# Two hybrid transformer blocks in float32: another order for VectorE and ScalarE at the front and the tail of each mixing

## The reference

```python
# per layer, both blocks
x = x + 0.5 * swiglu(rmsnorm(x), w_gate, w_up, w_down)      # width 2816
x = x + mixing(rmsnorm(x)) @ w_out
x = x + 0.5 * swiglu(rmsnorm(x), w_gate2, w_up2, w_down2)

# mixing of block 1: neighbourhood attention (8 heads) and gated linear attention (4 heads, two directions)
log_g = log_sigmoid(code @ w_gate + b_gate) / 16            # a cumulative sum of it is the decay
o = concat(rmsnorm(na(q, k, v)), rmsnorm(o_fwd + o_bwd) * silu(r))

# mixing of block 2: forgetting attention, dilated attention with rotary positions, HGRN2
log_f = logaddexp(log(lb), log(1 - lb) + log_sigmoid(z))    # z: the projection hf
k = (1 - lb) * sigmoid(-z);  q = silu(q_raw)                # q_raw: the projection hq
o = concat(fox, dilated, rmsnorm(hgrn2(q, k, v, log_f)) * sigmoid(g))
```

## Time and profile before

| | |
|---|---|
| three runs | 2106.34, 2108.96 and 2109.08 us; median 2108.96 |
| profiled execution, its own time | 2110.61 us |
| its span, first to last instruction | 2108.8 us |
| PE busy | 2048.7 us (97%) |
| DVE busy, ACT busy | 1310.0 us (62%), 1058.2 us (50%) |
| mean granted TensorE clock | 0.988 |
| DMA | 169 GB/s from HBM over the span |

### The profile page before, as it was taken

One profiled execution on the slowest core, in us unless ns is written; L12 is line 12 of the kernel. 1 busy time (PEld: TensorE's weight loads), 2 busy tenths in 40 slices (PEclk: granted clock), 3 DMA queues, 4 the chain that ended last, 5 costly groups with the idle time before them and its releaser, 6 DMA issues.

```text
span 2108.8 us, 26738 instructions
## 1 busy us (share of the span) xinstructions
PE 2048.7 (97%) x11144; PEld 1714.2 (81%) x11144; DVE 1310.0 (62%) x1532; ACT 1058.2 (50%) x1278; POOL 56.6 (3%) x72
## 2 busy tenths in 40 slices
PE   7999999999999999999999999999999999999998
PEld 5888877888888887788788888878888889887886
DVE  5655866555655686655565568765556556976554
ACT  4444565444544556544454456654454445565443
POOL 3200004000000000000000000000000000000000
PEclk9999999999999999999999999999999999999999
DMA  8654336555555433555455543345545554335551
GB/s 279 214 195 162 140 112 178 185 187 192 179 181 194 156 131 110 183 181 195 164 177 182 193 156 136 116 169 191 183 176 198 182 184 175 121 121 182 188 181 59
DMA packets 52217, 357.81 MB, mean 170 GB/s; under 512 B 6592, under 2 KB 7008, under 8 KB 9600
## 3 DMA queue, kind: packets, MB, share of 16 engines
q1 hardware_dynamic: 48960, 350.25, 46.6%
q0 software_dynamic: 2416, 5.51, 1.3%
q10 hardware_dynamic: 720, 0.34, 0.1%
HBM read 355.02 MB, written 1.05 MB: 169 GB/s over the span
## 4 chain that ended last, share of the span: by engine, by line
PE 88%; DVE 6%; ACT 3%; DVEq 1%; issue 1%; DMA 0%; ACTq 0%
PE bank L360 82%; DVE w_lo L1087 2%; PE bank L464 2%; PE bank L520 1%; PE bank L404 1%; ACT w_hi L747 1%; PE bank L601 1%; DVE h_lo L1104 1%; PE bank L566 1%; DMA cos_sin<-positions 0%; PE bank L587 0%; ACT h_hi L767 0%; DVEq L1275 0%; ACTq L920 0%; ACT arena L935 0%
## 5 line engine op out<-in xcount | busy, mean ns | idle before, releaser
L1087 DVE TENSOR_TENSOR w_lo<-raw,w_hi 128x2048 fp32r<-128x2048 f32 x332 | 762.7, 2297 | 387.8 <-ACT w_hi L747 387.4
L747 ACT ACTIVATE w_hi<-raw 128x2048 fp32r<-128x2048 f32 x332 | 634.3, 1911 | 270.9 <-PE bank L360 260.7
L360 PE MATMUL bank<-w_hi,h_hi 128*128 128x512 f32 x1536 | 611.7, 398 | 7.1 <-DVE w_lo L1087 4.1
L360 PE MATMUL bank<-w_hi,h_lo 128*128 128x512 f32 x1536 | 600.4, 391 | 0.0
L360 PE MATMUL bank<-w_lo,h_hi 128*128 128x512 f32 x1536 | 599.7, 390 | 0.0
L360 PEld LDWEIGHTS bank<-w_hi,h_hi 128*128 128x128 f32 x1536 | 289.4, 188 | 71.0 <-DVE w_lo L1087 10.2
L360 PEld LDWEIGHTS bank<-w_hi,h_lo 128*128 128x128 f32 x1536 | 289.0, 188 | 62.1
L360 PE MATMUL bank<-w_hi,act_hi 128*128 128x512 f32 x832 | 330.4, 397 | 6.3 <-DVE act_lo L1384 6.3
L360 PEld LDWEIGHTS bank<-w_lo,h_hi 128*128 128x128 f32 x1536 | 289.8, 189 | 56.5
L360 PE MATMUL bank<-w_lo,act_hi 128*128 128x512 f32 x832 | 326.1, 392 | 0.0
L360 PE MATMUL bank<-w_hi,act_lo 128*128 128x512 f32 x832 | 326.1, 392 | 0.0
(11 more groups left out here) (195 smaller groups left out, 1460.7 us busy)
## 6 DMA issues: line engine op xcount, KB each, us to landing
raw<-stream SPq DMA_DIRECT2D x332, 1024.0 KB, 4.8
arena<-rpb POOLq DMA_DIRECT2D x32, 96.0 KB, 9.3
x<-xt SPq DMA_DIRECT2D x4, 256.0 KB, 7.0
arena<-final_gain POOLq DMA_DIRECT2D x2, 512.0 KB, 4.5
out<-x SPq DMA_DIRECT2D x4, 256.0 KB, 2.8
arena<-c_level POOLq DMA_DIRECT2D x1, 384.0 KB, 3.4
arena<-code_w POOLq DMA_DIRECT2D x2, 128.0 KB, 3.6
arena<-c_att POOLq DMA_DIRECT2D x1, 256.0 KB, 5.0
```

The costliest lines, as they stand in the source:

```text
L360: last = mm(o, a, r, start=start and n == 0, stop=stop and n == len(pairs) - 1)
L747: fn(w_hi[u % SLOTS][:, :], raw[u % RAW][:, :], ACT.Copy).then_inc(hi_done, 1)
L1087: tt(w_lo[u % SLOTS][:, :], raw[u % RAW][:, :], w_hi[u % SLOTS][:, :].bitcast(F32), ALU.subtract).then_inc(lo_done, 1)
```

## The change

No instruction is added or left out but for drains and semaphores. The order changes:

1. Block 1, front: the logits (`gate_logits`) come ahead of the eviction of gq, the rest (`gate_sums`) behind the split of unit 3. The split of unit 4 moves behind `span_scale(0)` and `span_decay(1)`.
2. Block 2, front: turns 0 to 4 of DVE are one function, `hgrn_front`. Evictions and splits lie between the steps of the gate's chain, and the splits of units 6 and 7 behind all of it. ACT's order follows.
3. Tails: the split of unit i+3 in turn 10 or 13 comes early on both engines; `recurrence_rs` finishes its first half before the second; the transposes of item 7 go into the output unit, after its sixth of eight rows; block 1's `norm_sums` goes from after the fourth row of r = 1 to after the second.
4. Start of an FFN (six of the eight): `split(back 0)` stands between the pieces 1 and 2 of `turned_lo`, and `mean_square` behind piece 3.

```diff
@@ PE, mixing: output units
-                        between = None
+                        between = {}
                         if b == 1 and r == 0:
-                            between = lambda: recurrence_norm(b, L)
+                            between[0, 3] = lambda: recurrence_norm(b, L)
                         if b == 0 and r == 1:
-                            between = lambda: norm_sums(L)
+                            between[0, 1] = lambda: norm_sums(L)
+                        if TURN_AFTER[b].get(nunits + r) == 7:
+                            between[1, 1] = lambda: transposes(b, L, 7)
@@ ACT, recurrence_rs
                 for i in range(2):
                     fn(cum[:, 2 * i:2 * i + 2, :].rearrange("p a b -> p (a b)"), PX[i][:, :], ACT.Ln, bias=eps[:, :], scale=1.0 / P)
-                act.drain().then_inc(o_ln, 1)
-                for i in range(2):
+                    if i == 0:
+                        act.drain()
+                    else:
+                        act.drain().then_inc(o_ln, 1)
                     fn(cum[:, 2 * i:2 * i + 2, :], cum[:, 2 * i:2 * i + 2, :], ACT.Exp, scale=-0.5).then_inc(o_rs, 1)
@@ ACT, mixing
-                    late = i >= RECURRENCE_AFTER[b]
+                    late = i > RECURRENCE_AFTER[b]
...
+                    if b == 1 and i == 1:
+                        softplus(dec[:, :, :], qk2[:, 1, :, :], LAYERS + 2 * L + 1)
                     if not late:
                         split(mix_use(b, L, i + 3))
...
-                    if b == 1 and i == 2:
+                    if b == 1 and i in (1, 2):
+                        pair = slice(2 * (i - 1), 2 * i)
+                        act.wait_ge(evicted, plain_no(b, L, i + 1))
+                        fn(sig_tmp[1][:, pair, :], qk2[:, 0, pair, :], ACT.Exp, scale=-1.0)
+                    if b == 1 and i == 3:
                         act.wait_ge(gsilu, L + 1)
-                        fn(qk2[:, 1, :, :], qk2[:, 1, :, :], ACT.Exp)
                         fn(qks2[:, 0, :, :], qks2[:, 0, :, :], ACT.Exp)
                         act.drain()
                         fn(qks2[:, 0, :, :], qks2[:, 0, :, :], ACT.Ln, bias=1.0).then_inc(rg_done, 1)
-                    if name in ("hq0", "hq1"):
-                        pair = slice(2 * (i - 2), 2 * (i - 2) + 2)
-                        act.wait_ge(evicted, plain_no(b, L, i))
-                        fn(sig_tmp[1][:, pair, :], qk2[:, 0, pair, :], ACT.Exp, scale=-1.0)
-                    if name == "hq1":
+                        act.wait_ge(z_less, L + 1)
+                        fn(qk2[:, 1, :, :], qk2[:, 1, :, :], ACT.Exp).then_inc(z_exp, 1)
                         sigmoid(sig_tmp[1]).then_inc(sig_ready, 1)
@@ DVE, start of an FFN
-                    turned_lo(b, L, 2 * j, [1, 2, 3])
+                    turned_lo(b, L, 2 * j, [1])
+                    split(use_of("back", 0))
+                    turned_lo(b, L, 2 * j, [2, 3])
+                    mean_square(v)
                 else:
                     turned_lo(b, L, 2 * j, [0, 1, 2, 3])
-                mean_square(v)
-                split(use_of("back", 0))
+                    mean_square(v)
@@ DVE, gates
-            def gates(b, L):
-
-                tmp = qks1.rearrange("p a b t -> p (a b) t")
+            def gate_logits(L):
+
                 dve.wait_ge(z_ready, L + 1)
                 for c in range(4):
-                    ts(dec[:, c, :], PD[3 * (c // 2)][:, (c % 2) * T:(c % 2 + 1) * T], gain(b, L, "bias", c), None, ALU.add)
+                    ts(dec[:, c, :], PD[3 * (c // 2)][:, (c % 2) * T:(c % 2 + 1) * T], gain(0, L, "bias", c), None, ALU.add)
                 dve.drain().then_inc(logit_ready, 1)
+
+            def gate_sums(L):
+
+                tmp = qks1.rearrange("p a b t -> p (a b) t")
                 dve.wait_ge(softplus_ready, L + 1)
@@ DVE, in place of turns 0 to 4 of block 2
+            def hgrn_front(L):
+
+                z, mx, mn = qk2[:, 1, :, :], qks2[:, 1, :, :], qks2[:, 0, :, :]
+                evict(1, L, 0)
+                evict(1, L, 1)
+                dve.drain().then_inc(logit_ready, 1)
+                split(mix_use(1, L, 3))
+                dve.wait_ge(softplus_ready, LAYERS + 2 * L + 2)
+                stt(dec[:, :, :], z, 0.0, dec[:, :, :], ALU.min, ALU.subtract)
+                dve.drain()
+                tt(z, dec[:, :, :], z, ALU.subtract).then_inc(z_less, 1)
+                evict(1, L, 2)
+                split(mix_use(1, L, 4))
+                tt(dec[:, :, :], dec[:, :, :], wide(lb_all[:, L, 1, :, None], P, 4, T), ALU.add)
+                dve.drain()
+                tt(mx, dec[:, :, :], wide(lb_all[:, L, 0, :, None], P, 4, T), ALU.max)
+                evict(1, L, 3)
+                tt(mn, dec[:, :, :], wide(lb_all[:, L, 0, :, None], P, 4, T), ALU.min)
+                dve.drain()
+                tt(mn, mn, mx, ALU.subtract).then_inc(gsilu, 1)
+                split(mix_use(1, L, 5))
+                dve.wait_ge(rg_done, L + 1)
+                tt(mx, mx, mn, ALU.add)
+                dve.drain()
+                scans(4, mx, cum)
+                dve.wait_ge(z_exp, L + 1)
+                tt(z, z, wide(lb_all[:, L, 2, :, None], P, 4, T), ALU.mult)
+                dve.wait_ge(sig_ready, L + 1)
+                tt(qk2[:, 0, :, :], qk2[:, 0, :, :], sig_tmp[1], ALU.mult)
+                dve.drain()
+                base = decay_A[64:P, 0, 0, 0:64]
+                v.memset(bass.AP(tensor=base.tensor, offset=base.offset, ap=[base.ap[0], [4 * T + P, 2], [T, 4], [1, 64]]), 0.0)
+                span_scale(1, L, 0)
+                span_decay(1, L, 1)
+                evict(1, L, 4)
+                split(mix_use(1, L, 6))
+                split(mix_use(1, L, 7))
@@ DVE, mixing
-                    late = i in SPAN_AFTER[b] or item is not None or (b == 1 and i >= 3) or r >= 0
+                    opens = b == 0 and i + 1 in SPAN_AFTER[0] and SPAN_AFTER[0][i + 1] == 0
+                    late = i in SPAN_AFTER[b] or item is not None or r >= 0 or opens
+                    if b == 0 and i == 0:
+                        gate_logits(L)
...
                     if b == 0 and i == 0:
-                        gates(b, L)
...
+                        gate_sums(L)
...
+                    if i == RECURRENCE_AFTER[b]:
+                        split(mix_use(b, L, i + 3))
...
-                    if late:
+                    if late and i != RECURRENCE_AFTER[b]:
                         split(mix_use(b, L, i + 3))
```

More of the change, by code:

```diff
@@ L388, in row, with row_unit @@
                 return wide(PD[i][:, :], a_hi[:, kk, tok], a_lo[:, kk, tok], slice(kk * D + half * 512, kk * D + half * 512 + 512), u, start, stop)
-            def row_unit(u, a_hi, a_lo, first, between=None):
+            def row_unit(u, a_hi, a_lo, first, between={}):
                 ready(u)
@@ L395, in row_unit @@
                         last = row(u, i, kk, a_hi, a_lo, first and kk == 0, False)
-                    if kk == 0 and between is not None:
-                        between()
-                last.then_inc(used, 1)
+                        if (kk, i) == (1, 3):
+                            last.then_inc(used, 1)
+                        if (kk, i) in between:
+                            between[kk, i]()
             def turn(nn, source, half, t):
@@ L465, in turn_act, with down @@
                     last.then_inc(at_ready, 1)
-                def down(g, between=None):
+                def down(g, between={}):
                     pe.wait_ge(alo_ready, ffn_no(b, L, j, g) + 1)
@@ L677, in slot @@
                 item, turned = ITEM_AFTER[b].get(i), TURN_AFTER[b].get(i)
-                if turned is not None:
+                if turned is not None and turned < 7:
                     transposes(b, L, turned)
@@ L1447, in mixing @@
                     forget_sums(L)
-                for i in range(nunits + UNITS_OUT - 2):
+                    hgrn_front(L)
+                for i in range((0, 5)[b], nunits + UNITS_OUT - 2):
                     r = i - nunits
@@ L1487, in mixing @@
                         fox_tables(L)
[L1488 removed]
+                    if opens:
                         span_scale(b, L, 0)
```

39 lines of the change are left out of this document (3 added, 36 removed).

## The result

The changed kernel takes 2076.22 us (median of four executions, 2073.69 to 2077.44), the kernel before 2107.8 beside it. The ratio is 0.985, with a 95% interval of 0.9837 to 0.9863. The forecast was 2078, with a range of 2067 to 2090. The profiled execution has an own time of 2076.41 us and a span of 2074.6, against 2110.6 and 2108.8: 34.2 us less by either. The medians are 31.6 us apart; four executions of one kernel lie up to 3.8 us apart.

A forecast was written before the change was run, and what follows sets the result against it. PE, busy 97% of the span, was taken as the bound, gaining only at waits or low clock. Terms 10.2 + 4.4 + 11.8 + 1.4 + 3.6 = 31.4 us off 2110.6, adjusted to the median, gave 2078; range 2067 to 2090.

The forecast's parts named there:

- The new wait at the first `heads`: Block 1's front: PE waits 1.7 us behind DVE's decay and ACT's evictions and copy, taking back part of the gain.
- the fall from 3.2 to 2.2 us of lead: Block 2's front, after span step 1: PE is 3.2 us ahead of before, DVE only 2.2; 2.2 is counted.
- All six dips: Half-clock stretches of 6.83 us behind three long PE waits, each in two layers; their removal counted as 15.2 us before residues.
- rival (a): New PE waits in both fronts and block 1's tails pull the clock down again; 13.6 us for all six, 2091; chance 0.20.
- a border between 0.7 and 2.5 us: Length of PE wait above which the clock dips: none seen behind 0.7 us, one behind each 2.5 us.
- The rule of the Trainium skill that the forecast set aside: Prices each of six dips at half its 6.83 us, 3.4 us, 20.5 in all; the sum would be 5.3 us larger.
- Rivals (b) to (d): DVE catches up at once, 2062, 0.08; block 2's late split of unit 6 makes it slower, 2115, 0.03; nothing moves, 0.03.
- No residues: DVE catches up at once, so no new waits take back gains; parts give 46.8 us, 2062; chance 0.08.
- the residues: New PE waits in the fronts, among them 1.7 us in block 1, 2.3 and 1.3 in block 2, and 0.9 in block 1's tails.

The follow-up runs named there:

- the deferred exponential: Changed kernel with ACT's span exponential, in turns ahead of a pair unit, put behind the pair's evictions and the copy of the turned item; 2073.10 us, ratio 0.9846.
- The undone part: Changed kernel with the front of block 2's mixing put back to the old order of DVE and ACT; 2079.65 us, ratio 0.9866.
- the moved split: Changed kernel with block 2's split of unit 6 moved ahead of the wait for the forget gate's root; 2075.86 us, ratio 0.9853.
- the clearing: Changed kernel with the clearing of decay_A's upper corner in block 2's front moved from DVE to GpSimd; 2074.34 us, ratio 0.9848.
- the moved tables: Changed kernel with block 2's six bias-table operations on DVE moved behind the scale of span step 1; 2074.03 us, ratio 0.9846.
- the three edits: Changed kernel with the exponential deferred only at nvB and fvB, item 7's copy ahead of the squares, and decay_A's corner cleared on GpSimd; 2068.42 us, ratio 0.9818.

## Why the prediction was right, point by point

The unit starts of the two first profiles give what each part brought. The forecast's 31.4 us is near the 31.6 between the medians, and that is luck in part: the two profiled executions, from which its terms can be checked, are 34.2 apart.

| part | forecast, us | in the profile |
|---|---|---|
| front of block 1 | 10.2 | 5.6 + 5.5 = 11.0 |
| front of block 2 | 4.4 | 2.2 + 2.0 = 4.2 |
| tails of block 1 | 11.8 | 5.9 + 6.0 = 11.9 |
| tails of block 2 | 1.4 | 0.8 + 0.8 = 1.6 |
| FFN starts | 3.6 | 5.2 |
| first transfer, boundary, rest | none | 0.6 - 0.5 + 0.2 = 0.3 |
| sum | 31.4 | 34.2 |

- **Front of block 1.** 4.57 us for the wait and 2.26 and 2.13 for the clock, 6.8 where 6.4 was forecast. The new wait at the first `heads` took 1.25 back; 1.7 was forecast. It hung on DVE's decay and ACT's order behind it, as worked out, and the run with the deferred exponential showed that ACT's part could be removed.
- **Front of block 2.** Gross 6.9 and 7.0 (forecast 6.7). PE lost 2.47 and 2.83 up to fvA, 1.31 and 1.32 at span step 1, and 0.87 and 0.88 more up to dq: forecast 2.3, 1.3, and the fall from 3.2 to 2.2 us of lead. In the third mixing 1.5 of the 2.47 were a dip and only 0.91 the wait, in the fourth there was a wait of 2.76 and no dip; either way PE goes on when DVE's split of unit 6 ends. A dip ahead of such a wait costs nothing, since the wait is shorter by as much (2.47 us in all against 2.83). These are DVE's rows:

```profile
1261.77 4.48 DVE L1093 TENSOR_TENSOR w_lo<-raw,w_hi 128x2048 fp32r<-128x2048 f32 x2
1266.17 0.68 DVE L1347 TENSOR_TENSOR arena<-bank,rs 128x512 f32<-128x512 f32 x1
...
1270.35 0.68 DVE L1242 TENSOR_TENSOR arena<-arena 128x512 f32<-128x512 f32 x1
```

The first row is the splits of units 6 and 7. PE's fvA starts at 1264.11 behind the first, its span step at 1271.09 behind the last row. The undone part, the moved split, the clearing and the moved tables are the evidence that the stretch up to the span step is DVE's. The last 0.87 is not DVE's work alone, as the forecast had it when it took 2.2 us because item 0's softmax lies on DVE's queue: with ACT's exponential deferred and DVE unchanged, dq came 0.87 us earlier in both layers. ACT's exponential waits for DVE's decay, and the copy for `heads` stands behind it.
- **Tails.** 2.17 us for the wait (forecast 2.1), 2.96 for the clock and item 7 (3.2), 0.76 for the sums (0.6). That a wait of 0.8 us would leave the clock up was right.
- **FFN starts.** The term that was most mis-sized: 0.6 each, 0.87 measured, 1.6 us in all. The forecast took the listed wait, and the loss is the distance from start to start and the slow restart behind it. DVE's rows show the split in its new place, where DVE idled 1.52 us before:

```profile
337.00 2.28 DVE L1093 TENSOR_TENSOR w_lo<-raw,w_hi 128x2048 fp32r<-128x2048 f32 x1
339.19 1.65 DVE L1110 SCALAR_TENSOR_TENSOR h_lo<-bank,par_all,h_hi 128x256 fp32r<-128x256 f32 x4
```

- **The clock.** All six dips are gone from their places in both profiles of the changed kernel. Of rival (a) nothing is left there: the dip of 3.41 us in the third mixing lies ahead of the new wait. But what the forecast took for a border between 0.7 and 2.5 us is none. At unit fvA waits of 1.73 us (the clearing, third mixing), 1.75 (the three edits, third), 2.41 (the moved tables, third) and 2.79 (FFN starts undone, fourth) stand beside the start of a dip. Waits of 2.08 us (the clearing, fourth), 2.76 (the changed kernel, fourth: window 1778.80 to 1790.00) and, at the block boundary, 3.25 (the deferred exponential) left the granted clock at 1.00. Why one and not the other stays open, so that the new waits left the clock up in the changed kernel is luck in part. The 2.79 us beside a dip and the 2.76 us without one are the same wait in the same code, and the dip cost 0.65 us. The rule of the Trainium skill that the forecast set aside (TensorE: Matmul & The Clock Gate, Terms), throttled time by the share of pulses left out, would have made the sum 36.7, and 34.2 was measured. The clock's own part by the unit starts is 2.26 + 2.13 + 2.42 + 2.53 in the fronts and, less the 0.3 of item 7, some 2.6 in each tail: 14.5 us, where the forecast had 15.2 and the rule 20.5. For these dips, in which PE also stands still for 0.6 to 1.5 of the 6.83 us, the measurement speaks against the rule's full price.
- **Rivals (b) to (d)** are out. "No residues" would have given 46.8 us; the residues are 1.25, 4.7 and 5.0 us a layer and were measured one by one.

## What to carry to other kernels

When a wait is removed from a kernel that is nearly bound by PE, work out where the queue behind the releasing engine ends up next: here more than half of the gross gain of one front came back as three smaller waits, and the arithmetic of DVE's queue gave each to within 0.5 us. An operation that waits for another engine must not stand in a queue ahead of ones that are ready: deferring one exponential by three operations gained 1.25 us a layer at that place in block 1; where it then stood ahead of ready work again, 0.9 were lost. To relieve VectorE by GpSimd, try an operation that reads nothing first: here the clearing gained 0.67 us a layer, and the subtraction of two operands cost 5.

## What the runs showed of the hardware

- A wait of PE costs more than its listed length: 0.57 us listed, 0.70 from start to start, and 0.14 in the restart of the unit behind.
- The granted clock fell to 0.50 for 3.41 us behind `forget_rows` (1.99 us, eight matmuls with 4 of 128 rows), though PE waited for nothing. In nine of the fourteen profiles a dip of this length begins 0.1 to 1.5 us into unit fk, in three of them in the third mixing (the changed kernel twice, the front of block 2 undone) and in six in the fourth. That `forget_rows` is the cause is not shown: no run moved it.
- At the block boundary, with the same wait of 3.25 us in every profile, the stretch at half clock lasted 3.41, 6.83 or 10.24 us, and in one profile (the deferred exponential) there was none. The difference from 10.24 to 3.41 is worth 1.7 to 1.9 us, more than some of the edits tried.
- A GpSimd subtraction of 128x2048 took 4.72 us and stretched a DVE product of 128x1024 beside it from 1.22 to 5.58 us. A GpSimd clearing of 64x512 took 0.52 us and stretched nothing.
